# Feed-forward gate and up by Strassen's scheme in a two-block transformer kernel

## What is computed

```python
def swiglu(x, wg, wu, wd):
    return (jax.nn.silu(x @ wg) * (x @ wu)) @ wd      # wg, wu: 1024 x 2816, wd: 2816 x 1024

for l in range(DEPTH):                                # DEPTH = 2
    x = x + 0.5 * swiglu(rmsnorm(x, ffn1_norm[l]), ffn1_wg[l], ffn1_wu[l], ffn1_wd[l])
    h = rmsnorm(x, mix_norm[l]) @ w_in[l]
    ...
    x = x + o @ w_out[l]
    x = x + 0.5 * swiglu(rmsnorm(x, ffn2_norm[l]), ffn2_wg[l], ffn2_wu[l], ffn2_wd[l])
```

## Time and profile before

| | |
|---|---|
| median of the runs | 3082.9 us |
| profiled execution, span | 3080.3 us |
| TensorE, VectorE, ScalarE, GpSimd busy | 95%, 54%, 30%, 36% |
| chain that ended last | TensorE 80%, VectorE 7%, DMA 5% |
| mean granted TensorE clock | 0.982 of full |

### The profile page before, as it was taken

The page is one execution under the profiler, slowest core; times in us unless marked ns, Lnnn a source line. Parts: engine busy times, 40 slices in busy tenths (PEclk is TensorE's granted clock), DMA queues, the critical chain, the costliest instruction groups (busy, mean ns, idle before and its releaser), DMA issues.

```text
span 3080.3 us, 42571 instructions
## 1 busy us (share of the span) xinstructions
PE 2919.4 (95%) x16328; PEld 2226.9 (72%) x16328; DVE 1660.7 (54%) x2566; ACT 920.9 (30%) x1679; POOL 1121.9 (36%) x661
## 2 busy tenths in 40 slices
PE   7999999999999999999999999999998687999888
PEld 6888867678888888887676788888797676555444
DVE  7655675756555565556757655556556664112111
ACT  4222232543222232223225432223345751111111
POOL 3444354454434444443544544343443650000000
PEclk9999999999999999999999999999999888999999
DMA  5222222013222222221210132222230005999997
GB/s 206 101 84 102 82 83 83 1 37 128 83 102 102 82 103 102 83 102 71 109 47 2 56 129 83 102 102 80 82 124 22 21 18 214 405 424 423 423 424 318
DMA packets 45077, 411.47 MB, mean 134 GB/s; under 512 B 4992, under 2 KB 5248, under 8 KB 12032
## 3 DMA queue, kind: packets, MB, share of 16 engines
q1 hardware_dynamic: 44784, 408.03, 34.1%
q0 software_dynamic: 144, 1.38, 0.1%
HBM read 407.29 MB, written 2.10 MB: 133 GB/s over the span
## 4 chain that ended last, share of the span: by engine, by line
PE 80%; DVE 7%; DMA 5%; issue 3%; ACT 3%; POOL 1%; SPq 0%; DVEq 0%; ACTq 0%; POOLq 0%
PE banks L1642 10%; PE banks L1641 10%; PE banks L1640 10%; PE banks L1605 6%; PE banks L1474 5%; PE banks L1918 5%; PE banks L1651 5%; PE banks L1652 5%; PE banks L1653 5%; DMA experts<-moe_w 5%; PE banks L1553 3%; PE banks L1929 3%; PE banks L1689 2%; PE banks L1717 2%; PE banks L1702 2%
## 5 line engine op out<-in xcount | busy, mean ns | idle before, releaser
L2230 DVE SCALAR_TENSOR_TENSOR x<-banks,x 128x512 f32<-128x512 f32 x704 | 476.3, 691 | 416.5 <-PE banks L1653 416.5
L809 POOL TENSOR_TENSOR ffn_parts<-ring,ffn_parts 128x2048 fp32r<-128x2048 f32 x87 | 402.7, 4630 | 721.7 <-ACT ffn_parts L917 721.7
L1642 PE MATMUL banks<-x_parts_high,ffn_parts 128*128 128x512 f32 x672 | 263.8, 393 | 0.0
L1640 PE MATMUL banks<-h_lo,ffn_parts 128*128 128x512 f32 x672 | 262.8, 391 | 0.0
L1641 PE MATMUL banks<-x_parts_high,ffn_parts 128*128 128x512 f32 x672 | 262.8, 391 | 0.0
L1642 PE MATMUL banks<-h_hi,ffn_parts 128*128 128x512 f32 x672 | 262.2, 390 | 0.0
L1641 PE MATMUL banks<-h_hi,ffn_parts 128*128 128x512 f32 x672 | 262.0, 390 | 0.0
L1640 PE MATMUL banks<-x_parts_low,ffn_parts 128*128 128x512 f32 x672 | 261.8, 390 | 0.0
L917 ACT ACTIVATE ffn_parts<-ring 128x2048 fp32r<-128x2048 f32 x88 | 168.7, 1917 | 296.4 <-PE banks L1642 294.6
L814 POOL TENSOR_TENSOR ffn_parts<-ring,ffn_parts 128x1024 fp32r<-128x1024 f32 x88 | 211.4, 2402 | 103.8 <-ACT ffn_parts L923 103.8
L1918 PE MATMUL banks<-experts,mix 128*64 128x256 f32 x1520 | 189.1, 390 | 18.5 <-DMA experts<-moe_w 18.5
(11 more groups left out here) (395 smaller groups left out, 6575.6 us busy)
## 6 DMA issues: line engine op xcount, KB each, us to landing
ring<-ffn_w SPq DMA_DIRECT2D x87, 1536.0 KB, 6.5
experts<-moe_w SPq DMA_DIRECT2D x47, 2048.0 KB, 18.5
experts<-moe_w SPq DMA_DIRECT2D x48, 1024.0 KB, 19.1
ring<-mix_w SPq DMA_DIRECT2D x24, 1536.0 KB, 6.6
ring<-second_w SPq DMA_DIRECT2D x16, 1536.0 KB, 6.5
expert_table<-moe_w SPq DMA_DIRECT2D x16, 1024.0 KB, 15.0
expert_h<-moe_w SPq DMA_DIRECT2D x16, 1024.0 KB, 20.4
expert_table<-moe_w SPq DMA_DIRECT2D x16, 512.0 KB, 12.8
```

Source lines behind the costliest of these rows:

```text
L809: pool.tensor_tensor(s[:, 1], w, s[:, 0].bitcast(F32), ALU.subtract).then_inc(up_split, 1)
L1640: mm(bank[n % 2 + 2 * a], w[:, 0, a, k], lo[:, k], start=k == 0, stop=False)
L1642: last = mm(bank[n % 2 + 2 * a], w[:, 1, a, k], hi[:, k], start=False, stop=k == KC - 1)
L2230: V.scalar_tensor_tensor(x[:, q], bank[4 + q % 4], scale, x[:, q], ALU.mult, ALU.add).then_inc(down_used, c.one(down_used))
```

## The change

Feed-forward items are pairs of tiles now, 11 in each of the four feed-forwards; G counts pairs through the kernel, F feed-forwards, j pairs in one. The product of weights (two halves of 512 input features by two tiles) with x (those halves by two halves of 256 tokens) is made by the Strassen-Winograd form: 7 block products, for gate and for up, in place of 8. Operands of the weights are the four raw blocks and three sums (VectorE's sums makes four, one in place); operands of x are B11, B21, B22 and T1 to T4, the scaled x and differences of it, made at each start by x_gain and x_differences on GpSimd and make_t1 and make_t4 on VectorE, each with a high and a low part. Each operand is 128 x 1024. The products go to halves of banks 0 to 3; V1, V5 and C22 are parts of the result ("corners") that ScalarE copies or VectorE adds in SBUF. For the way down both tiles of a pair are added up in one bank: 8 adds to x for a pair. The loops are gone: each engine's list is written out. The raw blocks of a pair (2 MB) and its two halves of down weights (0.5 MB each) are loaded apart. The rotary tables are cut into six pieces, given to ffn as aside, and their three pairs of sines come at j = 7. Mixers, second block and experts keep their work. The lines that are left out are the buffers, the small split functions, the order of the first layer's start, and VectorE's and ScalarE's parts beside the output projection.

```diff
+        def load_pair(G):
+            last = [n for n in LAST_OF_RUN if n >= G][0]
+            if G < last:
+                sp.wait_ge(down_split, 2 * G + 1)
+                load_stage(G + 1, 0)
+            if G + 2 <= last:
+                sp.wait_ge(strassen, 2 * OPERANDS * (G + 1))
+                load_raw(G + 2)
+            if G < last:
+                sp.wait_ge(down_split, 2 * G + 2)
+                load_stage(G + 1, 1)
...
+        def x_gain(F, *list_):
+            for k in list_:
+                x_ready(pool, F, k)
+                kk = HALF * (k % 4)
+                dst = (UPPER if k < 4 else LOWER)[:, :, kk:kk + HALF]
+                pool.tensor_scalar(dst, two_halves(x[:, k]), col((COL_FFN1, COL_FFN2)[F % 2] + 8 * (F // 2) + k), 1.0,
+                                   ALU.mult, ALU.mult).then_inc(xg_ready, 1)
+        def x_differences(F):
+            pool.wait_ge(xg_ready, 8 * F + 8)
+            pool.tensor_tensor(T3, B22, B12, ALU.subtract).then_inc(t_pool, 1)
+            pool.wait_ge(x_low, lows_before(F) + 2)
+            pool.tensor_tensor(T2, B22, T1, ALU.subtract).then_inc(t_pool, 1)
...
+        def low(G, *list_):
+            for i in list_:
+                pool.wait_ge(w_high, OPERANDS * G + i + 1)
+                if G + i and i < 3:
+                    pool.wait_ge(sum_ready, 4 * G + (4 if i == 2 else 3))
+                if i == 4:
+                    pool.wait_ge(sum_ready, 4 * G + 4)
+                pool.tensor_tensor(operand_lo(G, i), OPERAND[G % 2][i], operand_hi(G, i).bitcast(F32), ALU.subtract).then_inc(w_split, 1)
...
+        def ffn(F):
+            for j in range(FFN_PAIRS):
+                G = FFN_PAIRS * F + j
+                if j == 0:
+                    low(G, 4)
+                    low_t3(F)
+                    low(G, 5)
+                    low_t4(F)
+                    low(G, 6)
+                else:
+                    low(G, 3, 4, 5, 6)
+                if G not in LAST_OF_RUN:
+                    low(G + 1, 0)
+                down_low(G, 0)
+                if G not in LAST_OF_RUN:
+                    low(G + 1, 1, 2)
+                down_low(G, 1)
+        def mixed(b, F):
+            lows, G = [j["piece"] for j in mixed_out(b)], FFN_PAIRS * F
+            for n in range(3, KC):
+                out_low(lows[n])
+                x_gain(F, n - 3)
+            x_gain(F, 5)
+            low(G, 0, 1)
+            x_gain(F, 6)
+            low(G, 2, 3)
+            x_gain(F, 7)
+            x_differences(F)
...
+        def high(G, *list_):
+            for i in list_:
+                n = OPERANDS * G + i
+                if i in (0, 2, 6):
+                    raw_landed(act, G, (0, None, 1, None, None, None, 3)[i])
+                else:
+                    act.wait_ge(sum_ready, 4 * G + (None, 1, None, 4, 3, 2)[i])
+                if n >= 4:
+                    act.wait_ge(strassen, 2 * n - 6)
+                act.activation(operand_hi(G, i), OPERAND[G % 2][i], ACT.Copy).then_inc(w_high, 1)
...
+        def corner(G, part, a):
+            act.wait_ge(strassen, 2 * OPERANDS * G + 2 * part + a + 1)
+            if part == 0:
+                act.activation(V1[G % 2][:, a], bank[a][:, 0:HALF], ACT.Copy).then_inc(corner_copied, 1)
+            else:
+                act.activation(V5[:, a], bank[a][:, HALF:T], ACT.Copy).then_inc(corner_copied, 1)
+        def silu(G, f):
+            act.wait_ge(gate_scaled, 2 * G + f + 1)
+            act.activation(GATES[f], GATES[f], ACT.Silu).then_inc(silu_ready, 1)
...
+        def ffn(F):
+            for j in range(FFN_PAIRS):
+                G = FFN_PAIRS * F + j
+                if j:
+                    high(G, 3)
+                    silu(G - 1, 1)
+                corner(G, 0, 0)
+                corner(G, 0, 1)
+                if j == 0:
+                    square(F, 7)
+                    high_t3(F)
+                    corner(G, 1, 0)
+                    high(G, 4)
+                    corner(G, 1, 1)
+                    high_t2(F)
+                    high_t4(F)
+                    high(G, 5)
+                    x_root(ACT.Silu)
+                    high(G, 6)
+                else:
+                    high(G, 4)
+                    corner(G, 1, 0)
+                    corner(G, 1, 1)
+                    high(G, 5, 6)
+                if G not in LAST_OF_RUN:
+                    high(G + 1, 0)
+                down_high(G, 0)
+                if G not in LAST_OF_RUN:
+                    high(G + 1, 1)
+                silu(G, 0)
+                if G not in LAST_OF_RUN:
+                    high(G + 1, 2)
+                if j == FFN_PAIRS - 1:
+                    silu(G, 1)
+                down_high(G, 1)
+                if F == 0 and j == 7:
...
+        def ffn(F):
+            for j in range(FFN_PAIRS):
+                G = FFN_PAIRS * F + j
+                inside = j and (4 if j == FFN_PAIRS - 1 else KC)
+                def product(i, at=None):
+                    w_hi, w_lo = operand_hi(G, i), operand_lo(G, i)
+                    v_hi, v_lo = (quarter(v[i]) for v in (X_HI, X_LO))
+                    pe.wait_ge(w_split, OPERANDS * G + i + 1)
+                    if j == 0:
+                        pe.wait_ge(x_high, highs_before(F) + (1, 2, 6, 6, 8, 7, 9)[i])
+                        if i < 5:
+                            pe.wait_ge(x_low, lows_before(F) + i + 1)
+                        else:
+                            pe.wait_ge(t_pool, 4 * F + i - 2)
+                        if i == 0 and F % 2:
+                            pe.wait_ge(taken_dve, OUT_TAKEN[F // 2] + KC)
+                    for a in range(2):
+                        if i == 0 and G:
+                            pe.wait_ge((gate_scaled, hidden_ready)[a], 2 * G - 1)
+                        if i in (1, 2):
+                            pe.wait_ge(corner_copied, 4 * G + 2 * i - 1 + a)
+                        if i == 4 and G:
+                            pe.wait_ge((gate_scaled, hidden_ready)[a], 2 * G)
+                        if i in (5, 6):
+                            pe.wait_ge(corner_added, 4 * G + 2 * i - 9 + a)
+                        o = bank[a + (2 if i > 3 else 0)][:, HALF:T] if i in (1, 3) else bank[a + (2 if i > 3 else 0)][:, 0:HALF]
+                        for k in range(KC // 2):
+                            s = slice(T * a + P * k, T * a + P * k + P)
+                            mm(o, w_hi[:, s], v_lo[:, k], start=i in (0, 4) and k == 0, stop=False, skip_group_check=True)
+                            mm(o, w_hi[:, s], v_hi[:, k], start=False, stop=False, skip_group_check=True)
+                            last = mm(o, w_lo[:, s], v_hi[:, k], start=False, stop=k == KC // 2 - 1, skip_group_check=True)
+                        last.then_inc(strassen, 1)
+                def down(G, *list_):
+                    g = HIDDEN[G % 2]
+                    for q in list_:
+                        if q == 0:
+                            pe.wait_ge(hidden_ready, 2 * G + 2)
+                        if q % 4 == 0:
+                            pe.wait_ge(down_split, 2 * G + 1 + q // 4)
+                        if KC * G + q > 3:
+                            pe.wait_ge(down_used, KC * G + q - 3)
+                        for f in range(2):
+                            s = slice(T * f + P * (q % 4), T * f + P * (q % 4) + P)
+                            w_hi, w_lo = W_DOWN_HI[q // 4][:, s], W_DOWN_LO[q // 4][:, s]
+                            mm(bank[4 + q % 4], w_hi, g[:, f, 1], start=f == 0, stop=False)
+                            mm(bank[4 + q % 4], w_hi, g[:, f, 0], start=False, stop=False)
+                            last = mm(bank[4 + q % 4], w_lo, g[:, f, 0], start=False, stop=f == 1)
+                        last.then_inc(down_ready, 1)
+                product(0)
+                product(1)
+                product(2)
+                if inside:
+                    down(G - 1, 0, 1)
+                product(3)
+                if inside:
+                    down(G - 1, 2, 3)
+                else:
+                    x_sums(FFN_SQUARES[F % 2][1])
+                product(4)
+                if inside == KC:
+                    down(G - 1, 4, 5)
+                product(5)
+                if inside == KC:
+                    down(G - 1, 6, 7)
+                product(6)
+                if inside == 4:
+                    down(G - 1, 4, 5, 6, 7)
+                    down(G, *range(KC))
...
+        def sums(G, *list_):
+            first, w = 4 * G, RAW[G % 2]
+            s1, s4, s2 = (EVEN_SUMS, ODD_SUMS)[G % 2]
+            for n in list_:
+                if n == 0:
+                    raw_landed(dve, G, 2, 3)
+                    V.tensor_tensor(s1, w[2], w[3], ALU.add).then_inc(sum_ready, 1)
+                elif n == 1:
+                    raw_landed(dve, G, 0)
+                    V.tensor_tensor(w[2], w[0], w[2], ALU.subtract).then_inc(sum_ready, 1)
```

(119 more changed lines are left out.)

632 lines of the change are left out of this document (341 added, 291 removed).

## The result

The changed kernel takes **3161.6 us** (median of four runs, 3157.8 to 3162.5) where the kernel before takes 3082.8: ratio 1.0252, 95% interval 1.0237 to 1.0266. It is slower, by 79 us. The profiled execution spans 3160.7 us, against 3080.3.

What follows compares the result with a forecast made beforehand. TensorE, busy for 95% of the span, was taken to bound the kernel. Stages: 1365.8 + 106.5 + 5.2 + 33.9 = 1511.4 us against 1457.9, +53.5, giving 3136 us, range 3056 to 3193.

Steps and rivals of the forecast that it cites:

- the stream: Feed-forward pairs on TensorE without waits: 31.04 us a pair, 44 pairs, 1365.8 us, 70.4 below before.
- the sines: Stage 1, ScalarE: six sines and two table loads of the rotary tables cost 4.2 us.
- the rival without one: Product matmuls of 256 columns take half of 0.2267, 0.1133 us: 49 us less, 3087; chance 0.04.
- Slips in the steady pair: Rival: second_gate or last_corner misses its margin, pairs take 33.7 us, 57 us more, 3193; chance 0.20.
- The starts: First two pairs of each feed-forward stage: TensorE waits for VectorE's and GpSimd's operands; 106.5 us lost in all.
- The walk: Step-by-step timing of engine queues from row prices, with VectorE and GpSimd excluding each other; gave 22.8 us in stages 2 and 4.
- The tables: Stage 1: six rotary table pieces ahead of second_gate delay product 1, plus sines and table loads: 33.9 us.
- The last down: End of each stage: the last way down waits some 1.3 us for the hidden parts, 5.2 in all.
- Cheap starts: Rival: queue holds fall on waits that are there anyway, 20 us below now, 3063 us; chance 0.21.

Runs made afterwards that it cites:

- Run 1: Kernel before, with nearly all gate and up matmuls of 512 tokens made as two of 256, same weights: 3126.0 us, ratio 1.0149.
- Run 10: Changed kernel with tables in nine pieces elsewhere, corner copies earlier, start orders changed, sum of squares and first pair's C22 in PSUM banks: 3115.5 us, ratio 1.0117.
- run 5: Changed kernel with matmuls that nobody reads put in TensorE's holes, in stage 1's table pairs and the starts of stages 2 to 4: 3157.9 us, ratio 1.0241.
- run 6: Changed kernel with ScalarE rounding product 6's operand ahead of the norm's root in the first pair of a run: 3170.3 us, ratio 1.0295.
- run 7: Changed kernel with three orders changed in the first pair: x chunks ahead of splits, B22's low part ahead of T4, stage 1 corner copies ahead of squares: 3164.0 us.
- Run 8: Changed kernel with only the running sum of squares moved to a free PSUM bank: 3151.6 us, ratio 1.0237.
- Run 9: Changed kernel, first pair of a run: C22 in a PSUM bank, first hidden tile ahead of last corners and fourth sum: 3147.7 us, ratio 1.0212.
- 11: Run 10's kernel with ScalarE's order mended, tables one pair later, mask copies apart, second sum behind first corners, stage 1 copies ahead of squares: 3099.7 us, ratio 1.0057.
- run 2: Changed kernel without the 33 vector instructions of the rotary tables in stage 1, sines kept: 3122.4 us, ratio 1.0139.

## Why the prediction was right, and where its sum was off

Forecast 3136 us, range 3056 to 3193, slower by over 0.2% with 0.69; measured 3161.6. It was slower, for the reasons given, and inside the forecast's own range of 3100 to 3170; the sum was 25 us too small, and two of its terms, the stream and the sines, erred the other way by 10 us together. Term by term (stages: 1511.4 predicted, 1535.7 measured):

- **The stream**, 31.04 us a pair: right; 30.89 in 25 pairs, 0.119 us a matmul and not 0.120. 6.6 us too much. Run 1 shows the fixed cost by itself, and the rival without one (3087) falls. The Trainium skill (TensorE: Matmul & The Clock Gate, section Back-to-back issue gap) counts 262 cycles for 256 columns, 109 ns. This kernel's rows say 119.
- **Slips in the steady pair**: none; the margins of 0.3 and 0.5 us held. Run 10 shows how thin they are: high parts in the wrong place in ScalarE's queue made every clean pair 0.65 us longer.
- **The starts**, 106.5: too small. Against 50.9 us for two clean pairs (20.0 + 30.9), and from the end of the work ahead, stage 1 loses 42.5 (37.5 predicted), the others 27.0, 26.5 and 27.1 (22.8, 23.4, 22.8): 123.1. The walk's places were right: product 1 behind the last x_gain (3.06 us), product 3 behind B22's low part (5.62), product 6 behind a split (2.07), the hidden parts (7.27); product 1 of the second pair began 49.0 us after the projection, not 45.8. Two things were mis-sized. The walk let several operations of VectorE in a row keep the port; in the trace GpSimd came in between, and each was held anew (T4, B22's low part, two additions; 1.21, 1.21 and 1.36 us when alone):

```profile
787.93 3.38 DVE L2469 TENSOR_TENSOR h<-mix 128x1024 f32<-128x1024 f32 x1 [2.29 <-POOL mix L907]
791.24 3.37 DVE L2473 TENSOR_TENSOR x_lo<-mix,lower_hi 128x1024 fp32r<-128x1024 f32 x1
794.53 5.64 DVE L2235 TENSOR_TENSOR mix<-mix 128x512 f32<-128x512 f32 x2
```

So T2's low part was done 25.9 us after the projection and not at 20.0, and product 4 began at 26.2, not 21.2; of this lateness 1.4 us were left at product 6 (34.4, 33.0). The other is the clock: in stage 2 the holes after the first matmul sum up to 20.3 us, and 37 matmuls at the 0.50 level behind two of them lost 4.0 more (5.4 in stage 3, 4.2 in stage 4, 7.5 in stage 1). The prediction had the row for it, said that holes can bring it back, and set it at nothing. How much of the first stretch reached the end of a start isn't shown; run 5 didn't keep the clock up there. In stage 1 the prediction also missed that the corner copies stand in ScalarE's queue behind squares that wait for VectorE's held additions: 16.8 us at product 1.

- **The tables**, 33.9: 43.0 in pairs 2 to 8. The holes were 5.57 us behind angles (6.50 with the mask copies) and 4.33 behind wraps, where 5.5 and 4.4 were predicted, the sines 0.75 instead of 4.2. Again the clock is what lacks, 1.5 to 2.1 us behind each of six holes, 10.2 in all (run 5 gave 1.7 back for each).
- **The last down**, 5.2: 7.6; stage 2's is 3.8, the others 1.26. Stream, starts, tables and this make 1532.9, 2.8 us under the measured sum; 1.6 of them are again the low clock, on eight matmuls behind stage 2's last hole.

With the low clock in the sum, 21.1 us in the four starts and 10.2 in the table pairs, the forecast would have been 3167 by my estimate from these rows, if none of it fell on waits that were there anyway. *Cheap starts* fell: GpSimd's idle share spoke for it, and run 6 shows that the part of it that lies in a start was no room.

**What the starts are bound by** was argued in the prediction as two engines that exclude each other, and walked as a chain. The chain found the places, but a chain suggests that a shorter link shortens it. Run 6 shortened a link and lost 9 us, run 7 gained nothing. Run 8 took SBUF operands away and nothing else: four additions went from 9.2 us to 3.2, and the kernel gained 10 us in the median, with executions in two groups. Run 9 gained 14, by an order and a bank together. Runs 10 and 11 have two orders and one time. So it is shown that VectorE's and GpSimd's joint use of SBUF makes single instructions of a start longer (3.4 us where 1.2 would do); that it sets the length of the start is what fits these runs best, and is not shown. How much of the 16.8 us that a start still loses would go with the remaining SBUF operands wasn't tried.

## What to carry to other kernels

A scheme that saves an eighth of the multiplications by halving the columns first pays a fixed cost for each instruction (0.006 us in 0.12, here 1.0 us of the 2.7 saved in a pair), and then needs a start, at each run, in which the helpers must make what TensorE consumes: with 11 pairs in a run, a gain of 1.75 us a pair can't carry a start of 25.
In-order queues turn a late instruction into a late stage: before work is put into an engine's idle time, follow what stands behind it, on that engine and on the next, down to TensorE. The same 33 instructions cost 39 us in one place and 4 in another, in smaller pieces.
A hole of TensorE should be priced with what follows it. And before an engine's idle time is counted as room, look whether VectorE or GpSimd, whichever is the other, has SBUF work in it: in run 6 2.4 us moved into 7.76 idle ones made a start 2.7 us longer.

## What the runs showed of the hardware that I had not expected

- A hole has a second price. Behind holes of 4.3 us and more the changed kernel's matmuls of 256 columns were 0.21 us apart and not 0.119 for 3.3 to 4.8 us (granted clock 0.50, the 1.2 GHz level). Shorter holes went either way: behind product 1's hole of 3.06 us in stages 2 and 4 the clock stayed at 1.00, but in run 2, behind the same hole in stage 4 (3.05 us), 16 matmuls were 0.21 us apart at 0.50, and in the changed kernel the clock was 0.50 behind the 1.92 us ahead of stage 3. Matmuls that nobody reads, put in the holes of stage 1's table pairs, kept the clock at 1.00 and gave 1.7 us back for each (run 5).
- VectorE's instructions with one SBUF operand can be held too: a TENSOR_SCALAR on 512 fp32 elements took 0.42 us or 2.4 to 2.6, while those that read a PSUM bank and one SBUF tile never took more than their own time (the 352 additions of the way down 0.67 to 0.69 us; run 8: 2.31 us for three).
- GpSimd's own time grows as well: a split of 2.40 us takes 3.3 to 3.4 where VectorE's SBUF work meets it. In run 8's stage 1 GpSimd's second difference and the split behind it took 2.36 and 2.38 us and not 2.78 and 2.81, but the three splits after them 3.1 to 3.4 and not 2.4 to 2.9: GpSimd as a whole gained nothing there.
